# The last three weight items of the gate projection as block products, interleaved with the merge of the delta-rule inverse

## What is computed

```python
h = rmsnorm(x, norm1_w)                                   # 288 tokens x 1024
proj = einsum('btd,de->bte', h, w_in)                      # 1024 -> 52 column chunks of 128
u_pool, u_qkv, b_raw, a_raw, z, gate_pool, gate_delta = split(proj, SPLITS)
...
t_inv = triangular_solve(eye + A, eye)                     # per head and chunk of tokens
...
merged = sigmoid(gate_pool) * branch_pool + sigmoid(gate_delta) * branch_delta
x = x + merged @ w_out
x = x + hier_moe(rmsnorm(x, norm2_w), ...)                 # 32 experts, all weights are read
```

## Time and profile before

| | |
|---|---|
| time, median of 3 runs | 576.82 us (575.82 to 578.66) |
| span of the profiled execution | 575.7 us; no other time of that execution is given |
| TensorE busy | 537.8 us, 93% of the span |
| weight loads of TensorE | 409.5 us, 71% |
| VectorE, ScalarE, GpSimd busy | 276.5, 152.8, 135.6 us |
| read from and written to HBM | 149.40 and 7.96 MB |

### The profile page before, as it was taken

How to read it: one execution, slowest core, us unless ns; L and a number is a source line. 1 busy time by engine, 2 the same in 40 slices (tenths; PEclk the granted TensorE clock), 3 DMA queues, 4 the chain that set the end, 5 groups by cost and what they waited for, 6 DMA issues and landing times. The chain is left out here.

```text
span 575.7 us, 13023 instructions
## 1 busy us (share of the span) xinstructions
PE 537.8 (93%) x5284; PEld 409.5 (71%) x5284; DVE 276.5 (48%) x803; ACT 152.8 (27%) x408; POOL 135.6 (24%) x218
## 2 busy tenths in 40 slices
PE   7999999999999999999999999999999959699974
PEld 6899999877788776779899888656455535265432
DVE  2767668782532626335766244534524231405045
ACT  3258465316851012133200123210111101010105
POOL 6587677013020081033224132000000000000001
PEclk9999999999999999999999999999998989889998
DMA  9735444657984154745387898899999999999992
GB/s 275 220 112 158 129 160 148 211 174 276 313 233 161 12 159 163 221 142 151 109 274 299 350 425 299 344 408 422 397 422 420 421 418 421 422 418 420 405 374 93
DMA packets 81229, 158.02 MB, mean 274 GB/s; under 512 B 11166, under 2 KB 65067, under 8 KB 68979
## 3 DMA queue, kind: packets, MB, share of 16 engines
q1 hardware_dynamic: 78604, 153.69, 72.8%
q10 hardware_dynamic: 2567, 3.51, 2.0%
HBM read 149.40 MB, written 7.96 MB: 273 GB/s over the span
## 5 line engine op out<-in xcount | busy, mean ns | idle before, releaser
L1426 PE MATMUL ps<-arena 128*128 128x288 f32 x480 | 122.6, 410 | 0.9 <-DVE arena L2341 0.7
L1426 PEld LDWEIGHTS ps<-arena 128*128 128x128 f32 x480 | 89.4, 190 | 26.5 <-issue 2.3
L2090 PE MATMUL ps<-arena 128*32 128x256 f32 x1024 | 64.7, 411 | 15.2 <-DMA arena<-in_w_up_dram 13.6
L1433 PE MATMUL ps<-arena 128*128 128x144 f32 x616 | 78.3, 287 | 0.0
L1433 PEld LDWEIGHTS ps<-arena 128*128 128x128 f32 x616 | 76.3, 190 | 2.4 <-issue 1.9
L2090 PEld LDWEIGHTS ps<-arena 128*32 128x32 f32 x1024 | 37.8, 118 | 40.1 <-issue 24.6
L906 POOL TENSOR_TENSOR arena<-arena 128x512 f32<-128x512 f32 x2 | 2.5, 1274 | 207.2 <-ACT arena L1339 207.2
L2366 DVE SCALAR_TENSOR_TENSOR ps<-arena,ps 128x312 f32<-128x312 f32 x72 | 39.1, 544 | 2.2 <-ACT ps L1026 0.9
L1379 PE MATMUL ps<-arena 128*128 128x128 f32 (+7 forms) x162 | 26.7, 284 | 7.4 <-DVE arena L3052 5.1
L2005 PE MATMUL ps<-arena 128*128 128x128 f32 x256 | 32.3, 279 | 0.7 <-DVE arena L3030 0.6
L2005 PEld LDWEIGHTS ps<-arena 128*128 128x128 f32 x256 | 29.8, 192 | 3.6 <-issue 2.5
(11 more groups left out here) (438 smaller groups left out, 807.9 us busy)
## 6 DMA issues: line engine op xcount, KB each, us to landing
arena<-in_w_gate_dram SPq DMA_DIRECT2D x32, 1024.0 KB, 12.9
arena<-in_w_up_dram SPq DMA_DIRECT2D x32, 1024.0 KB, 16.6
arena<-in_w_down_dram SPq DMA_DIRECT2D x28, 1024.0 KB, 17.0
arena<-in_w_in_dram SPq DMA_DIRECT2D x26, 1024.0 KB, 5.7
out_dram<-arena SPq DMA_DIRECT2D x9, 512.0 KB, 7.2
arena<-in_w_branch_delta_dram SPq DMA_DIRECT2D x4, 1024.0 KB, 5.8
arena<-in_w_out_dram SPq DMA_DIRECT2D x4, 1024.0 KB, 5.2
arena<-in_state_delta_dram SPq DMA_DIRECT2D x7, 512.0 KB, 8.5
```

What stands on the lines that cost most here:

```text
L1426: last = mm(ps[n % 2][:, 0:T], w[:, k, P * (n % 2):P * (n % 2) + P], hT[:, k, :], start=(k == 0), stop=(k == KD - 1))
L1433: last = mm(to[:, 0:HT], left[:, k, :], right[:, k, :], start=(first and k == 0), stop=(k == HK - 1), skip_group_check=True)
L2090: last = mm(to[CAP * e:CAP * e + CAP, 0:FE], xgT[:, k, CAP * e:CAP * e + CAP], w[e][:, k, :], start=(k == 0), stop=(k == KD - 1))
```

## The change

The items 23, 24 and 25 (chunks 46 to 51, `LATE_FAST`) are computed by the seven block products instead of by `proj`. Chunk 45 stays plain.

- TensorE: `late_products(i)` issues P1, P6, P5, P7 and `late_products_back(i)` issues P3, P4, P2. Only the banks 0 and 1 are used, in turn, so that nearly every product waits until the one before last has been read out of its bank. The halves of items 23 and 24 stand in different gaps of the merge; those of item 25 stand together at the end.
- VectorE: `sum_tokens` (five additions, inside `sample_values`, before it waits for the sample product) makes the four token sums anew, in slot 0 and at the end of the work area. Six additions for each item (`late_u2`, `late_u4`, `late_u7`, `late_sums_back`) are put between the merge's copies. The second `spread_v` goes away.
- ScalarE: a copy of P1 (`late_first`) for each item, and the six tanh now read the finished sums in SBUF and not a bank.
- GpSimd: `sum_weights` for the three items: the first before the wait for `sub_done`, the second after the scaling of the states, then the second `spread_v`, then the third. Its sums go to the slots 1, 4 and 1.
- SyncE: the slots of items 23 to 35 are dealt anew, `diagonal_blocks` stands after item 23 and not 24, `store_states(0)` after item 27 and not 29; the order of the slots for four gate weights of the experts follows.

```diff
+LATE_FAST = range(IN_ITEMS - 3, IN_ITEMS)
+BLOCKED = (*FAST, *LATE_FAST)
 SQUARES_AT = (2, 4, 7, 8)
 HT, HK = T // 2, KD // 2
 P1, P6, P5, P7, P2, P3, P4 = range(1, 8)
+L_P1, L_P6, L_P5, L_P7, L_P3, L_P4, L_P2 = range(1, 8)
+L_SUM2, L_SUM4, L_SUM7, L_SUM5, L_SUM6, L_SUM1 = range(1, 7)
 SUM2, SUM4, SUM7, SUM5, SUM6 = range(1, 6)
-SLOT_OF = [i % 4 if i < NQKV // 2 else i % RA for i in range(A_ITEMS)]
+SLOT_OF = [i % 4 if i < NQKV // 2 else i % RA for i in range(LATE_FAST[0])] + [5, 2, 3, 5, 2, 3, 4, 0, 1, 5, 2, 3, 4]
+LATE_SUMMED = 0
...
-    return 4 + i % 2
+    return (1, 4, 1)[LATE_FAST.index(i)] if i in LATE_FAST else 4 + i % 2
 def reader_ahead(i, s):
-    users = [j for j in range(i) if SLOT_OF[j] == s or (j in FAST and sums_slot(j) == s)]
+    users = [j for j in range(i) if SLOT_OF[j] == s or (j in BLOCKED and sums_slot(j) == s)
+             or (j in LATE_FAST and s == LATE_SUMMED)]
...
-STORE_AT = (IN_ITEMS + BP_ITEMS + 1, IN_ITEMS + BP_ITEMS + 3)
+STORE_AT = (IN_ITEMS + BP_ITEMS - 1, IN_ITEMS + BP_ITEMS + 3)
 MIX_BANK = (7, 4)
 CONV_AT = NQKV // 2 + RA
 ROWS_AT = NQKV // 2 + RA
-DIAG_AT = (N_GATE + 2) // 2 + RA - 1
-
-
-EVEN_GATES, ODD_GATES = (8, 9, 11, 12), (2, 3, 4, 5)
+DIAG_AT = LATE_FAST[0]
...
+EVEN_GATES, ODD_GATES = (8, 9, 11, 12), (5, 2, 3, 4)
...
+                if i in LATE_FAST:
+                    s, v = item_read(reader_ahead(i, sums_slot(i)))
+                    pool.wait_ge(s, v)
...
+            sum_weights(LATE_FAST[0])
             pool.wait_ge(S["sub_done"], 1)
             for h in range(H):
                 nc.gpsimd.tensor_tensor(state[h], state[h], eGd[:, h, :].unsqueeze(2).to_broadcast([P, BD, P]),
                                         ALU.mult).then_inc(S["sd_mul"], 1)
+            sum_weights(LATE_FAST[1])
+            pool.wait_ge(S["sdn_pe"], 2)
+            pool.wait_ge(S["decdve"], 8)
+            nc.gpsimd.tensor_tensor(vx, vnq[:, 1, :].unsqueeze(1).to_broadcast([P, BD, P]), spread(bmask4, P, P),
+                                    ALU.mult).then_inc(S["vx_done"], 1)
+            sum_weights(LATE_FAST[2])
...
+            def late_first(i):
+                act.wait_ge(S["proj"], product(i, L_P1))
+                nc.scalar.activation(late_gate(i, 0)[:, 0:HT], ps[0][:, 0:HT], ACT.Copy).then_inc(S["proj_free"], 1)
+            def late_tanh(i):
+                for odd, ready in ((1, L_SUM6), (0, L_SUM1)):
+                    act.wait_ge(S["sums"], late_added(i, ready))
+                    v = late_gate(i, odd)
+                    nc.scalar.activation(v, v, ACT.Tanh, scale=0.5).then_inc(S["proj_free"], 1)
             evac(LATE_GATES[0])
+            late_first(LATE_FAST[0])
             inner_copies()
-            evac(LATE_GATES[1])
             y_middle()
-            evac(LATE_GATES[2])
-            evac(LATE_GATES[3])
+            late_tanh(LATE_FAST[0])
+            late_first(LATE_FAST[1])
             y_outer()
-            evac(LATE_GATES[4])
+            late_tanh(LATE_FAST[1])
             outer_back()
-            evac(LATE_GATES[5])
-            evac(LATE_GATES[6])
+            late_first(LATE_FAST[2])
+            late_tanh(LATE_FAST[2])
...
+            def late_block(bank, left, right, opens=True):
+                for k in range(HK):
+                    last = mm(ps[bank][:, 0:HT], left[:, k, :], right(k), start=(opens and k == 0), stop=(k == HK - 1),
+                              skip_group_check=True)
+                last.then_inc(S["proj"], 1)
+            def late_left(i):
+                w = slots[SLOT_OF[i]].rearrange("p (k n) -> p k n", k=KD)
+                return w[:, 0:HK, 0:P], w[:, HK:KD, 0:P], w[:, HK:KD, P:2 * P]
+            def late_products(i):
+                a11, a12, a22 = late_left(i)
+                s1, s2, s3, s4 = [weight_sums(i)[:, j] for j in range(4)]
+                pe.wait_ge(ring_in[SLOT_OF[i]], 16 * loads_in(SLOT_OF[i], i + 1))
+                if i == LATE_FAST[0]:
+                    pe.wait_ge(S["proj_free"], free[2 * i - 1])
+                    pe.wait_ge(S["ht_done"], late_summed_by(5))
+                else:
+                    pe.wait_ge(S["sums"], late_added(i - 1, L_SUM1))
+                late_block(0, a11, lambda k: hT[:, k, 0:HT])
+                pe.wait_ge(S["pads"], weights_summed(i, 2))
+                late_block(1, s2, lambda k: late_summed[1][k])
+                pe.wait_ge(S["proj_free"], late_free(i, 1))
+                late_block(0, s1, lambda k: late_summed[0][k])
+                pe.wait_ge(S["pads"], weights_summed(i, 3))
+                pe.wait_ge(S["sums"], late_added(i, L_SUM2))
+                late_block(1, s3, lambda k: late_summed[2][k])
+            def late_products_back(i):
+                a11, a12, a22 = late_left(i)
+                s1, s2, s3, s4 = [weight_sums(i)[:, j] for j in range(4)]
+                pe.wait_ge(S["pads"], weights_summed(i, 4))
+                pe.wait_ge(S["sums"], late_added(i, L_SUM4))
+                late_block(0, s4, lambda k: hT[:, HK + k, HT:T], opens=False)
+                pe.wait_ge(S["sums"], late_added(i, L_SUM7))
+                late_block(1, a22, lambda k: late_summed[3][k], opens=False)
+                pe.wait_ge(S["sums"], late_added(i, L_SUM5))
+                late_block(0, a12, lambda k: hT[:, HK + k, 0:HT])
             inner_y()
             proj(LATE_GATES[0])
             inner_xx(0)
             state_unit(0)
             inner_xx(1)
-            proj(LATE_GATES[1])
+            late_products(LATE_FAST[0])
             state_unit(1)
             middle_y()
-            proj(LATE_GATES[2])
+            late_products_back(LATE_FAST[0])
             state_unit(2)
             middle_xx()
-            proj(LATE_GATES[3])
+            late_products(LATE_FAST[1])
             outer_y()
-            proj(LATE_GATES[4])
+            late_products_back(LATE_FAST[1])
             outer_xx()
-            proj(LATE_GATES[5])
             state_unit(3)
-            proj(LATE_GATES[6])
+            late_products(LATE_FAST[2])
+            late_products_back(LATE_FAST[2])
...
+            def sum_tokens():
+                b11, b12, b21, b22 = hT[:, 0:HK, 0:HT], hT[:, 0:HK, HT:T], hT[:, HK:KD, 0:HT], hT[:, HK:KD, HT:T]
+                dve.wait_ge(*item_read(reader_ahead(LATE_FAST[0], LATE_SUMMED)))
+                t1_, t2_, t3_ = [room_l[:, HT * HK * j:HT * HK * (j + 1)].rearrange("p (k t) -> p k t", k=HK) for j in range(3)]
+                V.tensor_tensor(t1_, b12, b11, ALU.subtract).then_inc(S["ht_done"], 1)
+                V.tensor_tensor(t3_, b22, b12, ALU.subtract).then_inc(S["ht_done"], 1)
+                dve.wait_ge(S["ht_done"], late_summed_by(1))
+                V.tensor_tensor(t2_, b22, t1_, ALU.subtract).then_inc(S["ht_done"], 1)
+                dve.wait_ge(S["ht_done"], late_summed_by(3))
+                for j, to in enumerate((room_l[:, 3 * HT * HK:3 * HT * HK + 2 * HT], room_w)):
+                    V.tensor_tensor(to.rearrange("p (k t) -> p k t", k=2), b21[:, 2 * j:2 * j + 2], t2_[:, 2 * j:2 * j + 2],
+                                    ALU.subtract).then_inc(S["ht_done"], 1)
+            def late_add(i, n, product_no, to, by, src, bank):
+                dve.wait_ge(S["proj"], product(i, product_no))
+                if n == L_SUM2:
+                    dve.wait_ge(S["proj_free"], late_free(i, 1))
+                if by:
+                    dve.wait_ge(S["sums"], late_added(i, by))
+                V.tensor_tensor(to, src, ps[bank][:, 0:HT], ALU.add).then_inc(S["sums"], 1)
+            def late_u2(i):
+                late_add(i, L_SUM2, L_P6, late_gate(i, 1)[:, 0:HT], None, late_gate(i, 0)[:, 0:HT], 1)
+            def late_u4(i):
+                late_add(i, L_SUM4, L_P5, late_gate(i, 1)[:, HT:T], L_SUM2, late_gate(i, 1)[:, 0:HT], 0)
+            def late_u7(i):
+                late_add(i, L_SUM7, L_P7, late_gate(i, 1)[:, HT:T], L_SUM4, late_gate(i, 1)[:, HT:T], 1)
+            def late_sums_back(i):
+                even, odd = late_gate(i, 0), late_gate(i, 1)
+                late_add(i, L_SUM5, L_P3, even[:, HT:T], None, odd[:, 0:HT], 0)
+                late_add(i, L_SUM6, L_P4, odd[:, 0:HT], L_SUM5, odd[:, 0:HT], 1)
+                late_add(i, L_SUM1, L_P2, even[:, 0:HT], None, even[:, 0:HT], 0)
             def sample_values():
                 dve.wait_ge(S["sd_pe"], 2)
                 link(V.tensor_tensor(tmpq, quads(ps[2][:, 2 * P:4 * P]), spread(nber4, P, P), ALU.mult))
                 link(V.tensor_tensor(oq, quads(ps[2][:, 0:2 * P]), spread(qs4, P, P), ALU.mult))
                 V.tensor_tensor(Rq, Rq, tmpq, ALU.add).then_inc(S["decdve"], 1)
+                sum_tokens()
                 dve.wait_ge(S["dec_pe"], 6)
                 last_as(V.tensor_copy(vnq, quads(ps[7][:, 0:2 * P])), "decdve", 8)
-            def spread_v(j):
-
-                if j >= 1:
-                    dve.wait_ge(S["sdn_pe"], 2 * j)
```

(19 more changed lines are left out.)

24 lines of the change are left out of this document (19 added, 5 removed).

## The result

Over 14 runs of each on one chip the changed kernel took 580.62 us (577.96 to 583.05) and the kernel before 577.26 us (575.82 to 579.18). The ratio is 1.005, with a 95% interval of 1.0039 to 1.0062, so the change costs 2.9 us (0.005 x 577.26). The forecast was +1.0. The prediction started from a median of 576.82 us; on that footing the changed kernel stands at 576.82 x 1.005 = 579.7, inside the range of 574.0 to 580.5. The median of these runs, 580.62, lies 0.1 above the end of that range, so that it is inside hangs on the footing. It is above the likeliest case's own range (576.5 to 579.2) and between the forecast and the slower rival (581.3).

What follows compares the result with a forecast made beforehand. TensorE, busy 93% of the span, was taken as the bound. The terms -3.1 + 1.4 + 0.2 + 2.1 + 0.4 = +1.0 us gave a forecast of 577.8 us, range 574.0 to 580.5.

Steps and rivals of the forecast that it cites:

- the likeliest case: Whole kernel: the forecast as laid out, +1.0 us, by itself 576.5 to 579.2 us; chance 0.49.
- the slower rival: Scan: GpSimd's delta-branch sums hold `scan_norm`, +3.9 us in place of 0.4, giving 581.3 us; chance 0.17.
- TensorE's saving and the hand-offs: Items 23 to 25: block products save 3.1 us; waits for banks to be read cost 1.4 us.
- ScalarE's last tanh: End of the new products: the tanh follows an addition, +0.4 us, about half of it slack, so +0.2 us.
- The recursion: Diagonal blocks: GpSimd's first weight sum holds VectorE's instructions at the shared port, a delay of 3.5 us.
- The rival in which the port costs nothing: Recursion: small products run beside GpSimd, stall only 0.2 us, nothing in the scan; -1.3 us, 575.5 us; chance 0.22.
- `inner_y`: TensorE behind the recursion: `inner_y` starts 2.1 us late after 1.46 us of slack; bounds 0.2 and 3.2 us.
- The queue: SyncE: `store_states(0)` moves to about 244 us, first `w_branch_delta` load to about 254, GpSimd's sums near 261 to 266.
- The scan: Head's norm: GpSimd's delta-weight sums hold two small instructions by 0.45 us each, less 0.5 slack: +0.4, upper bound 1.5 us.
- its point of decision: Scan: the slower rival decides once more than 2.3 us of its price reaches TensorE.
- The later sums and GpSimd's `spread_v`: After the eight scalings: `sum_weights(24)` takes 5 us, `spread_v` ends near 231 us, wanted at 234; cost nothing.

Runs made afterwards that it cites:

- e2_stores_early: The changed kernel with both stores of the sample states earlier in SyncE's queue (after items 25 and 27, not 27 and 31); ratio to the kernel before 1.0004.
- e3_reads_only: The kernel before, with four GpSimd additions after chunk 39 whose results nobody uses, and no block products; ratio to the kernel before 1.0046.
- e1_sum_after: The changed kernel with GpSimd's first weight sum moved behind the end of the recursion; ratio to the kernel before 0.9988.
- e4_filled: The changed kernel with eight idle 128x128 products on TensorE put before `inner_y`; ratio to the kernel before 1.0021.
- e6_again: The changed kernel repeated with no edit, as a control; ratio to the kernel before 1.0033.
- e5_both: The changed kernel with GpSimd's first weight sum behind the recursion and the states' stores earlier in SyncE's queue; ratio to the kernel before 0.9943.

## Why the prediction was right or wrong

The direction was right, and so was the mechanism of the largest forecast cost, the recursion held by GpSimd's reads. The size was short: +1.0 forecast, +1.9 to +2.9 measured, because a stop for instructions was overlooked and the scan's cost was put on the wrong sum. Step by step:

- **TensorE's saving and the hand-offs** (-3.1 + 1.4 = -1.7): the stage is 1.97 shorter. The net is right within 0.3. By the starts in TensorE's timeline, the three pairs hold the engine 22.41 us, 1.8 more than 3 x 6.87; 2.1 was forecast (0.7 for the ends, 1.4 for the waits). The two pieces without a wait in items 23 and 24 hold it 4.12 (224.08 to 228.20) and 3.14 us (241.85 to 244.99), 0.2 more than four and three products at 0.98. The two with a wait hold it 3.62 (230.40 to 234.02) and 4.55 (236.23 to 240.78), 0.68 and 0.62 more. So a wait costs 0.4 to 0.5, of which 0.2 is idle time, and the two together 0.9.
- **ScalarE's last tanh** (+0.2): nothing. With the delta sum out of the last norm, the scan takes 37.85 us in e2_stores_early, as in the kernel before.
- **The recursion** (3.5 us late): the last reduction ends at 205.61, 14.20 us after chunk 40's start. In the kernel before it ends at 203.64, 11.14 after that start, so it is 3.06 late (3.5 forecast). The pattern is the one laid out, each of the first two small products held by one addition of GpSimd's. `spread_v`, forecast at over 2 us, took 1.40: GpSimd's second addition had to wait for it, and not the other way round. The Trainium skill (SBUF — State Buffer, "Who interferes with whom") says that the instruction that gets the shared port pair first holds it for its whole length, and the trace agrees down to a single element (1.10 us). The rival in which the port costs nothing is dead: e3_reads_only shows the cost with nothing else changed.
- **`inner_y`** (+2.1): +1.69. The tiles of `X` land 22.04 us after chunk 40's start and 18.91 before the change, 3.13 late; less the slack of 1.46 that is 1.67.
- **The step that was mis-sized** is the end of that one: that the stall of `inner_y` is all that the late recursion costs. The slack of 1.46 us was `inner_y`'s alone. The chunk behind it stopped 0.59 us for its instructions already in the kernel before, and that stop ends a nearly fixed time after the tiles land, so it had no slack, and the delay comes back there: another 1.66. Together 3.35, which is the whole delay of the landing (3.13) and 0.2 more. The term was 2.1 and should have been 3.35. The stop stood in the trace before, between the rows shown in the earlier trace rows, with a second one of 0.61 at 221.58; I read these pieces by their starts and ends, and the prediction's reading that each piece starts where the last one ends, without a break, was wrong there.
- **The queue** came as laid out: stores at 245.50 (244 forecast), the first delta load at 254.31 (254), GpSimd's sum from 261.03.
- **The scan** (+0.4): +1.38. The first delta sum, on which I had put the 0.4, costs TensorE nothing (in e1_sum_after and e4_filled it does: waits of 0.28 and 0.66 stand beside it, with small instructions of a norm at 1.01 and 0.92 us). The second one costs 1.38. I had not followed it: it stands behind GpSimd's preparations, and these behind the landing of the stores that had been moved. Two instructions held for 0.81 and 0.58, each more than the 0.45 of the estimate, in the last head, which has no slack. This is the slower rival's mechanism at a third of its price, and its point of decision (2.3 us in TensorE) was not reached.
- **Sum by measured terms**: -1.97 + 0 + 3.35 + 1.38 = +2.76. The later sums and GpSimd's `spread_v`, forecast at nothing, cost nothing that a row shows (its `spread_v` ends at 231.35, forecast near 231).

**Settled by the runs:** that GpSimd's reads make the first two terms (e3_reads_only, e1_sum_after), that the place of the second delta sum makes the third (e2_stores_early), and that the clock doesn't make the stop in chunk 45 (e6_again). **Well supported:** that the stop is a transfer of instructions behind bulk loads: by moving the loads, which brings the transfer from about 4 us to 1 us after the landing of `X`, by moving the stop with the count of instructions, and by a constant 2.46 to 2.66 us. **Open:** when such a transfer is asked for isn't in the trace, so its wait in the queue is known only by that comparison; why e5_both gains the last 0.56 too; and why the tiles land 1.5 us later in the two kernels with idle products.

## What to carry to other kernels

Before GpSimd gets new work, look at what VectorE does in that stretch: one addition of 1.27 us holds even a one-element instruction, and in a chain of small instructions each of the additions is paid in full. A slack is a slack of one instruction; follow a delay past it to the next wait, "issue" included, and follow a moved store to all who wait for its landing. An edit that costs more than it saves may be saved by the place of its parts: here two moves of whole blocks turned a loss of 1.9 to 2.9 us into a gain of 3.3.

## What the runs showed of the hardware

- TensorE's instructions come in pieces of 16 KB over the same 16 DMA engines as the data. When 2 to 3 MB of loads are in front, TensorE stops for "issue" with its operands ready: 0.37 to 1.74 us in chunk 45, 2.33 in `inner_xx`. At all these stops it goes on 2.3 to 2.7 us after the piece's transfer starts.
- A small stop comes without loads too: in e1_sum_after the DMA engines are 4% busy from 217 to 219 us, the next piece starts at 219.12, 1.2 us after the end of the stop before it, and TensorE, which runs through the 127 records of small products in between, stops 0.34 us until 221.57.
- A VectorE product of one element took 1.10 us beside GpSimd's additions, and a scaling of four elements 0.97 in the scan; GpSimd's own addition took 2.14 when VectorE came first. A reduction (one input) between them kept its 0.15, at 195.86, while GpSimd's fourth addition ran; but the scalings, with one input too, were held.
- In this stretch the granted clock fell to the lower level in two of the twelve profiles: in the changed kernel's first at 215.0 us, after TensorE had idled 1.63 us, and in e3_reads_only's at 221.0, after idle times of 1.52 and 1.62. It stayed at 1.00 in e6_again and e2_stores_early, after 1.61 and 1.65, and 1.54 and 1.74. In the first, slow products filled the stop that followed, and the chunk's length is explained without the clock; in e3_reads_only no stop hid it, and pieces that took 7.34 us in the kernel before took 7.99.
